# Moving 32 expert up projections into the top-k stage, all modulation chunks into the gate stage, and widening the other up projections

## Time and profile before

| what | us |
|---|---|
| median of 3 runs | 2290.24 (2286.39 to 2290.87) |
| the profiled execution, its own time | 2286.94 |
| its span, first to last instruction | 2285.1 |
| wq stage, about | 220 to 292 |
| modulation groups beside the rest of the top-k | 296 to 373 |
| gate stage | 380 to 507 |
| experts | 512 to 1240 |
| second block | 1240 to 2285 |

### The profile page before, as it was taken

The page is one execution under the profiler, slowest core; times in us unless marked ns, Lnnn a source line. Parts: engine busy times, 40 slices in busy tenths (PEclk is TensorE's granted clock), DMA queues, the critical chain, the costliest instruction groups (busy, mean ns, idle before and its releaser), DMA issues.

```text
span 2285.1 us, 37329 instructions
## 1 busy us (share of the span) xinstructions
PE 2206.0 (97%) x13410; PEld 1893.8 (83%) x13410; DVE 1242.4 (54%) x1820; ACT 956.4 (42%) x1312; POOL 92.8 (4%) x50
## 2 busy tenths in 40 slices
PE   8999898999999999999999999999899999999998
PEld 6999723559999999999998888878788889898997
DVE  4557888985555555555557433322644444255554
ACT  5644311234444444444455323212433335336653
POOL 0000002650000000000000000000000000000000
PEclk9999999999999999999999999999999999999999
DMA  6434365436555556555554322232233335254553
GB/s 215 138 131 144 113 221 194 132 129 199 187 189 184 188 188 202 187 189 184 188 189 149 111 92 92 97 100 96 70 103 100 110 111 192 91 187 146 181 188 101
DMA packets 95689, 343.14 MB, mean 150 GB/s; under 512 B 10930, under 2 KB 12594, under 8 KB 95252
## 3 DMA queue, kind: packets, MB, share of 16 engines
q1 hardware_dynamic: 94532, 337.35, 44.4%
q0 software_dynamic: 1104, 5.05, 0.7%
HBM read 341.31 MB, written 1.05 MB: 150 GB/s over the span
## 4 chain that ended last, share of the span: by engine, by line
PE 88%; DVE 8%; issue 2%; ACT 1%; DMA 0%; DVEq 0%; POOL 0%; ACTq 0%; POOLq 0%
PE ps L1316 19%; PE ps L1317 19%; PE ps L1318 19%; PE ps L1539 5%; PE ps L1540 5%; PE ps L1541 5%; PE ps L1513 3%; PE ps L1478 3%; PE ps L1347 2%; PE ps L1348 2%; PE ps L1349 2%; PE ps L1671 1%; PE ps L1356 1%; DVE WL L786 1%; PE ps L1720 1%
## 5 line engine op out<-in xcount | busy, mean ns | idle before, releaser
L786 DVE TENSOR_TENSOR WL<-RAW,WH 128x1024 fp32r<-128x1024 f32 x565 | 683.2, 1224 | 665.1 <-ACT WH L409 661.0
L1316 PE MATMUL ps<-XH,WH 128*128 128x256 f32 (+1 forms) x2648 | 803.2, 303 | 29.7 <-DVE WL L786 16.2
L409 ACT ACTIVATE WH<-RAW 128x1024 fp32r<-128x1024 f32 x565 | 586.4, 1055 | 538.2 <-PE ps L1318 342.1
L1317 PE MATMUL ps<-XL,WH 128*128 128x256 f32 (+1 forms) x2648 | 794.5, 300 | 0.0
L1318 PE MATMUL ps<-XH,WL 128*128 128x256 f32 (+1 forms) x2648 | 794.2, 300 | 0.0
L1316 PEld LDWEIGHTS ps<-XH,WH 128*128 128x128 f32 x2648 | 511.8, 193 | 58.0 <-issue 20.5
L1317 PEld LDWEIGHTS ps<-XL,WH 128*128 128x128 f32 x2648 | 512.8, 194 | 20.3 <-issue 1.2
L1318 PEld LDWEIGHTS ps<-XH,WL 128*128 128x128 f32 x2648 | 512.5, 194 | 14.5
L1539 PE MATMUL ps<-WH,AH 128*128 128x512 f32 x512 | 200.8, 392 | 0.0
L1540 PE MATMUL ps<-WH,AL 128*128 128x512 f32 x512 | 200.7, 392 | 0.0
L1541 PE MATMUL ps<-WL,AH 128*128 128x512 f32 x512 | 199.2, 389 | 0.0
(11 more groups left out here) (255 smaller groups left out, 2257.4 us busy)
## 6 DMA issues: line engine op xcount, KB each, us to landing
RAW<-in_wstream SPq DMA_DIRECT2D x637, 512.0 KB, 3.8
H<-in_xT SPq DMA_DIRECT2D x1, 1024.0 KB, 4.8
CTX<-in_ctxT POOLq DMA_DIRECT2D x1, 1024.0 KB, 7.6
HX<-in_ctxT POOLq DMA_DIRECT2D x1, 1024.0 KB, 5.9
DIST<-in_dist POOLq DMA_DIRECT2D x1, 1024.0 KB, 5.2
out<-HX SPq DMA_DIRECT2D x2, 512.0 KB, 3.3
MASK<-in_mask POOLq DMA_DIRECT2D x1, 512.0 KB, 3.9
DFTL<-in_dftl POOLq DMA_DIRECT2D x1, 512.0 KB, 3.7
```

Of the source, the lines that this page charges most:

```text
L409: act.activation(WH[:, slot, :], RAW[:, slot, :], ACT.Copy).then_inc(hi_ready, 1)
L786: dve.tensor_tensor(WL[:, slot, :], RAW[:, slot, :], WH[:, slot, :].bitcast(F32), ALU.subtract).then_inc(lo_ready, 1)
L1316: pe.matmul(dst, wh, xh, start=start, stop=False, skip_group_check=not check)
L1317: pe.matmul(dst, wh, xl, start=False, stop=False, skip_group_check=not check)
```

## The change

- `PRE` = 32 rows of experts, rows 96 to 127, have their up chunks done in the top-k stage, right after wq (*pre*, 32 chunks). ACT puts gelu(x . u) into rows 96 to 127 of `G`. The last four of them come after the transposes of `SEL`.
- POOL, not DVE, makes `WL` for the last 14 wq chunks and all pre chunks. DVE's top-k has no splits any more.
- All 72 ada chunks are in the gate stage, 2 or 3 per unit in units 0 to 29. `CS` is now 128 x 32, zero beyond its 2 columns, and the matmul of input part `k` writes output rows 32 (k mod 4) to 32 (k mod 4) + 31; k and k + 4 are accumulated. Each group's 128 x 512 result is copied to `MROW`, turned by four 128 x 128 transposes, and DVE adds up the four partial sums (`row_sum`).
- POOL has no work in the gate stage. DVE makes `OI` with its gates in 8 instructions of 128 elements and multiplies rows 96 to 127 of the result into `G` (`gated_rows`).
- Experts: 2 ups, then 32 downs alone, then 94 pairs whose up is *wide*: 8 matmuls of 512 columns (high weights x [high input, low input], side by side in `XHL`) and 8 of 256 (low weights x high input). ACT copies the low-input half out of PSUM (`up_rest`) and DVE adds it (`up_sum`) ahead of the gelu.

```diff
+PRE = 32
+PRE_ROW = NKEYS - PRE
+NE = NKEYS - PRE
+UNITS = T // 8
+ADA_UNITS = UNITS - 2
     ("wq", 16),
+    ("pre", PRE),
     ("ada", MODB),
-    ("peer", 256),
+    ("peer", 256 - PRE),
+def ada_through(n):
+    return min(MODB, (n + 1) * MODB // ADA_UNITS)
+def turn_after(done):
+    return done // 4 - 1 if done >= 6 and done % 4 == 2 else None
...
 pool:
-            with pool.Fori(0, T // 16) as it:
-                for q in range(2):
-                    pool.wait_ge(s["oi_ready"], at(q + 1, 2, it))
-                    pool.tensor_tensor(OI[:, q, :, :], OI[:, q, :, :],
...
+            pool.wait_ge(lo_ready, C0["wq"] + 2)
+            for c in range(C0["wq"] + 2, ADA):
+                pool.wait_ge(hi_ready, c + 1)
+                pool.tensor_tensor(WL[:, c % 4, :], RAW[:, c % 4, :], WH[:, c % 4, :].bitcast(F32),
+                                   ALU.subtract).then_inc(lo_ready, 1)
...
 act:
+            for i in range(PRE):
+                c = C0["pre"] + i
+                if i and c + 2 < ADA:
+                    split_hi(c + 2)
+                act.wait_ge(chunk_done, c + 1)
+                act.activation(G[:, PRE_ROW + i, :], ps[:, (U_PRE + i) % 4, 0:T],
+                               ACT.Gelu_apprx_tanh).then_inc(ring_evac, 1)
...
+            def up_rest(e, it=None):
+                act.wait_ge(chunk_done, at(PQ + 2 * (e - 1) + 1, 8, it))
+                act.activation(UT[:, e % 2, :], ps[:, e % 4, T:2 * T], ACT.Copy).then_inc(s["up_half"], 1)
...
 dve:
-                for j in range(4):
-                    split_lo(C0["wq"] + j + 2, it, 4)
-                    if j:
-                        top(j - 1, it, 1, it * 2 + 2)
+                for part in range(3):
+                    top(part, it, 1, it * 2 + 2)
...
+            def onehots(n):
+                q, tok = n % 2, slice(8 * n, 8 * n + 8)
+                if n < 2:
+                    dve.wait_ge(chunk_done, ADA - 1 + n)
+                else:
+                    dve.wait_ge(s["onehot_used"], n + 1)
+                dve.tensor_tensor(OJ[q][:, :, :], IOTA[:, :].unsqueeze(1).to_broadcast(wide),
+                                  SLT[:, 1, tok].unsqueeze(2).to_broadcast(wide), ALU.is_equal)
+                for t in range(8):
+                    own = slice(8 * n + t, 8 * n + t + 1)
+                    ins = dve.tensor_scalar(OI[q][:, t, :], IOTA[:, :], SLT[:, 0, own], SLT[:, 2, own],
+                                            ALU.is_equal, ALU.mult)
+                ins.then_inc(s["onehot_ready"], 1)
...
+            def up_sum(e, it=None):
+                dve.wait_ge(s["up_half"], at(e - 1, 4, it))
+                dve.tensor_tensor(ps[:, e % 4, 0:T], ps[:, e % 4, 0:T], UT[:, e % 2, :], ALU.add).then_inc(s["up_sum"], 1)
...
 pe:
+            with pe.Fori(0, PRE // 4 - 1) as it:
+                for i in range(4):
+                    pre_up(i, it)
+            pe.wait_ge(s["sc_ready"], 16 + 4)
             pe.wait_ge(s["sel_ready"], 1)
...
+            for i in range(PRE - 4, PRE):
+                pre_up(i)
+            def mod_chunk(i):
+                c, bank = ADA + i, 6 + (i // 4) % 2
+                pe.wait_ge(landed[c % 4], 16 * (c // 4 + 1))
+                for kk in range(2):
+                    k = 2 * (i % 4) + kk
+                    rows = slice(32 * (k % 4), 32 * (k % 4) + 32)
+                    ins = pe.matmul(ps[rows, bank, :], CS[:, k, :], RAW[:, c % 4, kk * 512:kk * 512 + 512],
+                                    start=(k < 4), stop=(k >= 4))
+                ins.then_inc(chunk_done, 1)
+            def turn_row(g):
+                pe.wait_ge(s["mrow_ready"], g + 1)
+                if g:
+                    pe.wait_ge(s["row_summed"], g)
+                for i in range(4):
+                    ins = pe.transpose(ps[:, 5, i * P:i * P + P], MROW[:, g % 2, i * P:i * P + P], IDP[:, :])
+                ins.then_inc(s["row_turned"], 1)
...
+            pe.wait_ge(ring_evac, U_GATES)
+            for n in range(UNITS):
+                q = n % 2
+                pe.wait_ge(s["onehot_ready"], n + 1)
+                pe.wait_ge(s["g_ready"], n + 1)
+                pe.wait_ge(s["gm_ready"], n + 1)
+                for t in range(8):
+                    ins = pe.matmul(ps[:, 2 * q + t // 4, (t % 4) * P:(t % 4) * P + P], OJ[q][:, t, :], OI[q][:, t, :],
+                                    start=True, stop=True)
+                ins.then_inc(s["onehot_used"], 1)
+                while done < ada_through(n):
+                    if done >= 8 and done % 4 == 0:
+                        pe.wait_ge(s["mrow_ready"], done // 4 - 1)
+                    mod_chunk(done)
+                    done += 1
+                    if turn_after(done) is not None:
+                        turn_row(turn_after(done))
+            turn_row(MODB // 4 - 1)
...
+            def up_wide(e, c, it=None):
+                split_ready(c, it, 8)
+                both = ps[:, e % 4, :].rearrange("p (a t) -> p a t", a=2)
+                for k in range(KB):
+                    w = slice(k * P, k * P + P)
+                    pe.matmul(both, WH[:, c % 4, w], XHL[:, :, k, :], start=(k == 0), stop=(k == KB - 1),
+                              skip_group_check=True)
+                    ins = pe.matmul(ps[:, e % 4, 0:T], WL[:, c % 4, w], XH[:, k, :], start=False, stop=(k == KB - 1),
+                              skip_group_check=True)
+                ins.then_inc(chunk_done, 1)
...
             def pair(e, it=None):
                 if e >= 2:
                     pe.wait_ge(s["gated_ready"], at(e - 1, 4, it))
-                up(e + 2, PC + 2 + 2 * e, it)
-                down(e, PC + 3 + 2 * e, it, first=it is None and e == 0)
+                up_wide(e + 2, PQ + 2 + 2 * e, it)
+                down(e, PRE + e, PQ + 3 + 2 * e, it)
```

More of the change, by code:

```diff
@@ L554, in _ @@
             act.activation(LGD[:, 2, :], LGD[:, 1, :], ACT.Ln, bias=ONES[:, 0:1]).then_inc(s["lgd_ready"], 1)
[L556 to L574, removed]
-            act.sem_inc(s["g_ready"], 2)
@@ L577, in _ @@
[L577 to L585, removed]
@@ L590, in expert_hi, with pre_hi @@
+            PC = C0["peer"]
+            PQ = PC + PRE
+            def pre_hi(i, it=None):
+                if it is not None or i >= 2:
+                    act.wait_ge(chunk_done, at(PC + 2 + i - 2 + 1, 4, it))
+                src = G[:, PRE_ROW + i, :] if it is None else G[:, bass.ds(it * 4 + (PRE_ROW + i), 1), :]
+                dst = AH[:, i % 2, :] if it is None else AH[:, i % 2, :].unsqueeze(1)
+                act.activation(dst, src, ACT.Copy).then_inc(s["a_hi"], 1)
             def expert_hi(e, it=None):
@@ L620, in _ @@
             tmp_c, xh_c = TMP16[:, :, C_], XH2_16[:, :, C_]
-            for e in range(CTX_E, 126):
+            for e in range(CTX_E, NE - 2):
                 pair(e)
@@ new lines, in _ @@
+            dve.sem_inc(s["gm_ready"], 2)
+            onehots(0)
+            dve.wait_ge(ring_evac, U_GATES)
+            for n in range(UNITS):
+                if n + 1 < UNITS:
+                    onehots(n + 1)
+                gated_rows(n)
+                if n >= 1:
+                    for done in range(ada_through(n - 2) + 1 if n >= 2 else 1, ada_through(n - 1) + 1):
+                        if turn_after(done) is not None:
+                            row_sum(turn_after(done))
+            PC = C0["peer"]
@@ new lines, in _ @@
+            done = 0
+            for n in range(UNITS):
+                q = n % 2
[10 more added lines that the diff above has]
+                    mod_chunk(done)
+                    done += 1
+                    if turn_after(done) is not None:
+                        turn_row(turn_after(done))
@@ L1548, in _ @@
             pe.wait_ge(s["mod_ready"], 1)
+            down(0, 0, PC + 2, first=True)
+            with pe.Fori(0, PRE // 4 - 1) as it:
+                for i in range(1, 5):
+                    down(i, i, PC + 2 + i, it, 4)
+            for i in range(PRE - 3, PRE):
+                down(i, i, PC + 2 + i)
             def pair(e, it=None):
```

296 lines of the change are left out of this document (156 added, 140 removed).

## The result

The changed kernel took 2218.78 us (median, 2217.13 to 2222.61) against 2288.57 for the kernel before (2286.39 to 2290.87), 0.9697 of it with an interval of 0.9679 to 0.9716. The forecast was 2221.0. The total was met to 0.1%, but two of its four terms were wrong, by 23 and 17 us, in opposite directions.

A forecast was written before the change was run, and what follows sets the result against it. It took PE to bound the experts and the gate stage, DVE the top-k and look-up. Terms -96.5 - 5.1 + 26 + 10 = -65.6 us took 2286.9 to 2221; range over cases 2184 to 2280.

The forecast's parts named there:

- term 3: Gate stage: 153 us against 127, +26, with the 72 modulation chunks only partly overlapping on PE.
- term 4: Start of the gate stage: +10, as POOL's splits slow DVE's two-input instructions; upper end +29.
- likeliest case: Gate stage with paired records, the forecast itself: 2221 us, 2207 to 2240 by the ends of term 4; chance 0.46.
- full overlap: Gate stage: chunks of one burst run side by side, about 128 us, +1 for +26; total 2196; chance 0.20.
- the prediction's own signs: Forecast wrong if modulation runs serially or in parallel, PE waits for WL in pre stage, or DVE exceeds 4.8 us per unit.
- Term 1: Experts: 94 wide ups of 2.79 us replace 125 narrow ones of 2.87 behind the first down, -96.5 us.
- Term 2: Hand-over from gate stage to the first down: 10.8 us in place of 15.9, -5.1.
- no-overlap rival: Gate stage: every modulation record waits for the one before, +78 us; total 2273; chance 0.24.
- POOL as the pace: Pre chunks: POOL's splits at 4.3 us delay the gate stage, +46 for +10; sign turns at 3.8; chance 0.07.
- The upper end of +29: Start of the gate stage: all of some 24 two-input and copy instructions of DVE suffer beside POOL, +29 us.

The follow-up runs named there:

- narrow_ups: The changed kernel with the 94 wide ups of the experts made narrow again, without up_rest and up_sum: 2221.0 us, 0.9708 of the kernel before.
- half_loads: The changed kernel loading only the first half of each modulation chunk, 256 KB in place of 512: 2209.33 us, timed once.
- one_group: The changed kernel with all eight input parts of a modulation chunk written to one group of 32 output rows, not four: 2288.87 us.
- late_exp: The changed kernel with ACT's exponential of the values moved from behind pre up 20 to behind pre up 27: 2221.11 us, 0.971 of before.

## Why the prediction was right, and where it was not

**The total** was right by luck, by compensation: +26 forecast and +3 measured in term 3, +10 forecast and +26.7 measured in term 4. The likeliest case's own range (2207 to 2240) held the result for a wrong reason. The case that came true, full overlap (0.20), had 2182 to 2215 and missed it, as its term 4 was too small as well. By two of the prediction's own signs the forecast is wrong: the modulation runs in parallel, and PE waits for `WL` in the pre stage (11.4 us).

- **Term 1, experts.** The count was right: 31 ups of 2.87 us are 89.0, narrow_ups shows 89.9 (717.0 less 627.1), and PE was busy all the time, 624 of 624 us. The failed step is "8 x (0.229 + 0.12) = 2.79", by its size: the saving was put at 0.08 per up, 7.5 us in all, and narrow_ups measured 2.6. The up itself came out near it, at 2.81, but the price of a down was taken from a stream in which it follows narrow matmuls, and it rose from 2.75 to 2.78. The added work of ACT and DVE was hidden, as forecast.
- **Term 2, hand-over.** Forecast 10.8, measured 9.1 us. PE's granted clock was at its upper level (1.00) under the two ups, whose matmuls start 0.12 us apart, so the 1.9 us for half clock, put in by analogy to the kernel before, were not due. From the last one-hot to the first up it took 3.3 us, against 3.2 forecast for ACT's copy and the two parts of the split.
- **Term 3, gate stage.** The failed step is the premise "the two records of one matmul share their rows and can't overlap, but the second can run beside the first of the next matmul". In the trace as many records start together as there are groups (four, two or one), and the next ones follow some 0.45 us later. Read so, the second record of a matmul does not hold back the matmuls on other groups; the trace does not name records first or second, so this is read from their number. The full-overlap rival was the right one: its 128 us against 129.9, held by the loads (half_loads), with PE and DVE 11 us behind. What argued for it stood in the working, "nothing in the diff orders them otherwise". The Trainium skill's statement (TensorEngine Tiling (Array Packing), Key Properties) that tiles run their matmuls in parallel agrees with the trace, 3.62 us on one group against 1.07 on four, a factor of 3.4 here. The no-overlap rival was built as one_group, forecast 2273 and measured at 2288.87; its stage took 198 us against 205 in the rival's sum, so the rest of the difference is the late start of the stage, which the forecast had too small.
- **Term 4, start of the gate stage.** The failed step is "if only two-input instructions suffer": copies and casts do as well (0.20 to 2.20, 0.18 to 1.86), and make up 14 of the 22.4 us of the top-k; the sums there cost 8.4, near the 9.3 put on them. The collisions were put at 9.3 + 7.7 = 17.0 us and cost 22.4 + 10.3 = 32.7. The -14 for the splits that DVE gave away was right (14.2). So the softmax began 15.7 us later than forecast (390.34 against 374.6). From there on it was +1.4 (16.2 against 14.9): the first of the four ups ran at half clock and took 4.1 us instead of 2.9. The upper end of +29 held the value, and the rule of the Trainium skill (SBUF — State Buffer, Who interferes with whom, on the shared port pair) that copies are hit was the better guide than the nearest row: the copies and casts above bear it out. The prediction had cited it and put +20 beside its own +10.
- **POOL as the pace** did not happen. A split took 2.40 us alone and 3.7 beside the old look-up; over all 46 the mean is 2.6, against the 3.8 at which the sign would turn. PE's 11.4 us of waiting for `WL` lay inside DVE's longer chain; late_exp took 9.4 of them away and gained nothing.

What stays open: the top-k's tiles were not moved, so whether its 22.4 us can be got back as those of the look-up were is not shown. Nor is it shown why some of its copies and casts were slowed and others of the same shape were not.

## What to carry to other kernels

When work is moved from VectorE to POOL, where the two collide on operands in SBUF, price each moved instruction by what it does to VectorE's chain: here 46 splits of 2.4 us on POOL cost VectorE some 33 us, more than the 14 us it had gained by giving 12 of its own away. With the look-up's tile in PSUM the contention there was gone, 10.3 us, at a price of 2.4 us for the halves. And where matmuls with few output columns are put on separate row groups of the output, look at once for the next bound, here the loads: the gain from two groups to four was 8 us, from one to two 62.

## What the runs showed of the hardware

- Plain fp32 matmuls that write different groups of 32 output rows run side by side, two records each: eight records in 1.07 us on four groups, 1.91 on two, 3.62 on one.
- VectorE reading one operand from PSUM and one from SBUF ran at its full 1.23 us for 1024 elements beside POOL, and POOL beside it at 2.4; with both in SBUF they took 4.33 for 2.29 and 3.7 for 2.4. Beside POOL memsets of the same tile, which have no inputs, no two-input instruction was slowed (`CAND` 0.41), but casts (0.59 on average for 0.20) and the `STG` copies (0.60 for 0.42) were.
- In the one case tried, another order moved the collisions and did not reduce them: with the exponential later, five long look-up instructions became two (6.2 us less) and the look-up began 5.4 us later.
